# Value products of a sparse and of a memory attention, 256 columns wide in place of 128

## The reference, cut to what matters

```python
def _dsa(...):                      # sparse attention: 8 heads of 128, 2 key-value heads
    ...
        logits = jnp.where(valid[:, :, None, None, :], logits, -jnp.inf)
        p = jax.nn.softmax(logits, axis=-1).astype(v.dtype)
        o = jnp.einsum('bqgrk,bqkgd->bqgrd', p, vg)
...
def _memory_attn(...):              # memory attention: 4 heads of 256 over 256 memory rows
    ...
    logits = jnp.einsum('bthd,bmhd->bhtm', q, k).astype(jnp.float32)
    p = jax.nn.softmax(logits, axis=-1).astype(v.dtype)
    o = jnp.einsum('bhtm,bmhd->bthd', p, v)
```

## Time and profile before

| | us |
|---|---|
| median of 3 runs | 1372.25 (1372.23 to 1376.3) |
| the profiled execution | 1372.86 |
| its span (first to last instruction) | 1371.0 |
| PE busy | 1292.2 (94% of the span) |
| DVE, ACT, POOL busy | 636.5, 636.3, 416.4 |
| sparse attention's steps, about 736 to 853 | 160 value records |
| memory attention's steps, about 974 to 1029 | 128 value records |

### The profile page before, as it was taken

The page is one execution under the profiler, slowest core; times in us unless marked ns, Lnnn a source line. Parts: engine busy times, 40 slices in busy tenths (PEclk is TensorE's granted clock), DMA queues, the critical chain, the costliest instruction groups (busy, mean ns, idle before and its releaser), DMA issues.

```text
span 1371.0 us, 16957 instructions
## 1 busy us (share of the span) xinstructions
PE 1292.2 (94%) x6321; PEld 1000.1 (73%) x6321; DVE 636.5 (46%) x1414; ACT 636.3 (46%) x1107; POOL 416.4 (30%) x211
## 2 busy tenths in 40 slices
PE   5999989889989999999999998999899999999996
PEld 4798666467768767776877786888787777777674
DVE  3265353643320135237897444314334133678785
ACT  5453534353552647445333545333434323477772
POOL 4273232024663421333333222444105431100003
PEclk9999999999999999999999999999999999999999
DMA  5233333133444221222322111342107430799945
GB/s 165 66 115 100 120 119 109 50 101 115 147 119 168 74 80 32 62 77 66 104 85 72 52 54 55 115 153 83 33 1 251 180 151 20 306 409 409 420 185 202
DMA packets 76461, 179.13 MB, mean 131 GB/s; under 512 B 11200, under 2 KB 22774, under 8 KB 69718
## 3 DMA queue, kind: packets, MB, share of 16 engines
q1 hardware_dynamic: 68672, 164.96, 35.1%
q0 software_dynamic: 2592, 8.40, 1.6%
q10 hardware_dynamic: 5110, 4.62, 1.2%
HBM read 152.79 MB, written 25.17 MB: 130 GB/s over the span
## 4 chain that ended last, share of the span: by engine, by line
PE 71%; DVE 8%; ACT 3%; issue 3%; POOL 1%; DMA 0%; DVEq 0%; ACTq 0%; POOLq 0%
PE ps L1064 17%; PE ps L1065 17%; PE ps L1066 17%; PE ps L1602 4%; PE ps L1470 1%; PE ps L1453 1%; PE ps L1586 1%; PE ps L1230 1%; DVE mix_lo L2557 1%; DVE work L2788 1%; PE ps L1426 1%; DVE best L2786 1%; PE ps L1573 1%; PE ps L1498 1%; PE ps L1460 1%
## 5 line engine op out<-in xcount | busy, mean ns | idle before, releaser
L931 POOL TENSOR_TENSOR w_lo<-raw,w_hi 128x1024 fp32r<-128x1024 f32 (+1 forms) x158 | 377.8, 2405 | 733.5 <-ACT w_hi L1829 724.8
L1064 PE MATMUL ps<-w_hi,act_hi 128*128 128x512 f32 (+1 forms) x560 | 234.2, 418 | 5.5 <-DVE probT_m L3224 2.3
L1829 ACT ACTIVATE w_hi<-raw 128x1024 fp32r<-128x1024 f32 (+1 forms) x158 | 159.9, 1033 | 170.0 <-PE ps L1066 161.5
L1065 PE MATMUL ps<-w_lo,act_hi 128*128 128x512 f32 (+1 forms) x560 | 219.7, 392 | 0.0
L1066 PE MATMUL ps<-w_hi,act_lo 128*128 128x512 f32 (+1 forms) x560 | 219.1, 391 | 0.0
L1064 PE MATMUL ps<-w_hi,mix_hi 128*128 128x512 f32 x320 | 131.9, 412 | 4.9 <-DVE mix_lo L2557 3.6
L1064 PEld LDWEIGHTS ps<-w_hi,act_hi 128*128 128x128 f32 (+1 forms) x560 | 104.7, 187 | 43.2 <-issue 12.5
L1066 PE MATMUL ps<-w_hi,mix_lo 128*128 128x512 f32 x320 | 127.0, 397 | 0.0
L1065 PE MATMUL ps<-w_lo,mix_hi 128*128 128x512 f32 x320 | 126.9, 397 | 0.0
L1066 PEld LDWEIGHTS ps<-w_hi,act_lo 128*128 128x128 f32 (+1 forms) x560 | 104.4, 186 | 25.1
L1065 PEld LDWEIGHTS ps<-w_lo,act_hi 128*128 128x128 f32 (+1 forms) x560 | 104.6, 187 | 24.4 <-issue 1.8
(11 more groups left out here) (477 smaller groups left out, 2116.1 us busy)
## 6 DMA issues: line engine op xcount, KB each, us to landing
raw<-in_w_in SPq DMA_DIRECT2D x92, 512.0 KB, 3.6
gu<-in_w_gate SPq DMA_DIRECT2D x16, 1024.0 KB, 7.7
gu<-in_w_up SPq DMA_DIRECT2D x16, 1024.0 KB, 10.0
dn<-in_w_down SPq DMA_DIRECT2D x16, 1024.0 KB, 10.2
x_rows<-zeros SPq DMA_DIRECT2D x16, 512.0 KB, 4.9
raw<-in_w_out SPq DMA_DIRECT2D x16, 512.0 KB, 4.5
raw<-in_w_mem_kv SPq DMA_DIRECT2D x16, 512.0 KB, 3.8
xe<-x_rows SPq DMA_DIRECT2D x15, 512.0 KB, 10.4
```

The costliest lines, as they stand in the source:

```text
L931: pool.tensor_tensor(lo[:, 0:a], raw[:, g % RAW_SLOTS, 0:a], hi[:, 0:a].bitcast(F32), ALU.subtract).then_inc(*POOL.done(("w_lo", g)))
L1064: pe.matmul(dst, l_hi, r_hi, start=start, stop=False, skip_group_check=skip)
L1065: pe.matmul(dst, l_hi, r_lo, start=False, stop=False, skip_group_check=skip)
L1829: nc.scalar.activation(split_slot(g)[0][:, 0:a], raw[:, g % RAW_SLOTS, 0:a], ACTF.Copy).then_inc(*ACT.done(("w_hi", g)))
```

## The change

Two turns now share one value product, 256 columns wide.

- In the sparse attention the order of turns becomes the one of `turn_of`: pairs of heads, and within a pair row block 0 of both heads, row block 1 of both, and so on. Turns j = 2m and 2m + 1 are the two heads of pair m // 4 at row block m mod 4. Both have the same key-value head, so the same value block is the weight for both. The value product m stands in step 2m + 4, where the one of turn 2m + 1 stood; odd steps have none.
- `d_probT` becomes two buffers of two turns each, and bank 7 holds two heads by two row blocks; ACT copies it out every second value product (line 2253 of the new file).
- In the memory attention the order of turns stays. The value product of two neighbouring row blocks of a head is issued where the one of the odd row block stood; the even one's step issues nothing on PE. `m_probT` becomes two buffers of two turns each.
- `mix_dsa` of two heads is laid in when a pair of heads ends.

The multiplications and the shape of scores, transposes, exponentials and divisions are the same ones.

```diff
@@ -297,14 +297,14 @@
     n = NT * DSA_H
     steps = []
     for j in range(n + 3):
-        steps += [[("dsa_values", j - 3)] * (j >= 3) + [("dsa_turn", j - 2)] * (2 <= j < n + 2) + [("dsa_scores", j)] * (j < n)]
+        steps += [[("dsa_values", j // 2 - 2)] * (j >= 4 and j % 2 == 0) + [("dsa_turn", j - 2)] * (2 <= j < n + 2) + [("dsa_scores", j)] * (j < n)]
     done, ended, fresh = [], False, 0
     dense = item("gate01", "w_o01", "gate10")
     for step in [x for s in spread(steps, [[p] for p in dense[:-4]]) for x in s]:
         order += [step]
         ended = ended or step == ("part", "w_o01", KC // 2 - 1, NT - 1)
         if step[0] == "dsa_values" and step[1] % NT == NT - 1:
-            done += [("mix_dsa", step[1] // NT)]
+            done += [("mix_dsa", 2 * (step[1] // NT) + i) for i in range(2)]
             fresh = 2
         elif ended and step[0] == "dsa_turn":
             if done and (len(done) > 1 or not fresh):
@@ -484,7 +484,7 @@
         dv = sb("dv", [P, NT, 256], SC + 49.5)
         d_mask = sb("d_mask", [P, 1280], SC + 53.5)
         rel = sb("rel", [P, 2, SEQ], SC + 58.5)
-        d_probT = sb("d_probT", [P, 2, SEQ], SC + 58.5)
+        d_probT = [sb(f"d_probT{i}", [P, NT, 2, P], SC + at) for i, at in enumerate((58.5, 68.5))]
         d_sq = sb("d_sq", [P, 2, 512], SC + 62.5)
         ik2 = sb("ik2", [P, NT, P], SC + 66.5)
         d_prob = sb("d_prob", [P, 3, SEQ], SC + 62.5)
@@ -503,7 +503,7 @@
         mem_lo = sb("mem_lo", [P, KC, MEM], SC + 28, F32R)
         mqT = sb("mqT", [P, 8, SEQ], SC + 41.5)
         m_prob = sb("m_prob", [P, 3, MEM], SC + 57.5)
-        m_probT = sb("m_probT", [P, 2, MEM], SC + 60.5)
+        m_probT = [sb(f"m_probT{i}", [P, 2, 2, P], SC + at) for i, at in enumerate((60.5, 70.5))]
 
         zeros = sb("zeros", [P, 256], SC + 71.75)
         xs_ffn = sb("xs_ffn", [P, NT, D], SC)
@@ -873,7 +873,7 @@
                         sp.dma_start(mem_vals, mv_new[:, :, :].rearrange("p c n -> p (c n)")).then_inc(mem_spilled, 16)
                     if names[g] == ("mem_q0", 0):
                         sp.wait_ge(mem_spilled, 32)
-                        sp.wait_ge(*PE.after("d_O", NT * DSA_H - 1))
+                        sp.wait_ge(*PE.after("d_O", NT * DSA_H // 2 - 1))
                         sp.wait_ge(*DVE.after("mix_lo", "dsa", DSA_H - 1))
                         sp.dma_start(mkT[:, :, :].rearrange("p c n -> p (c n)"), mem_keys).then_inc(mem_back, 16)
                         sp.dma_start(mv[:, :, :].rearrange("p c n -> p (c n)"), mem_vals).then_inc(mem_back, 16)
@@ -1447,7 +1447,7 @@
                                         [("dqn", n, t) for t in range(NT)])
 
             def dsa_scores(j):
-                h, t = divmod(j, NT)
+                _, t, h, _ = turn_of(j)
                 n = P * (t + 1)
                 claim(4 + j % 2, (DVE, ("d_max", j)))
                 pe.matmul(ps[:, 4 + j % 2, 0:n], dqT[:, h, P * t:P * t + P], dkT[:, h // DSA_G, 0:n], start=True,
@@ -1456,20 +1456,21 @@
             def dsa_turn(j):
                 pe.wait_ge(*DVE.after("d_norm", j))
                 claim(6, (ACT, ("d_PT", j)))
-                for b in range(j % NT + 1):
+                for b in range(turn_of(j)[1] + 1):
                     tr = pe.transpose(ps[:, 6, P * b:P * b + P], d_prob[:, j % 3, P * b:P * b + P], ident[:, :])
                 tr.then_inc(*PE.done(("d_PT", j)))
 
-            def dsa_values(j):
-                h, t = divmod(j, NT)
-                g = h // DSA_G
-                pe.wait_ge(*ACT.after("d_PT", j))
-                if t == 0:
-                    claim(7, (ACT, ("d_out", h)))
+            def dsa_values(m):
+                p, t = divmod(m, NT)
+                g = 2 * p // DSA_G
+                for i in range(2):
+                    pe.wait_ge(*ACT.after("d_PT", 2 * m + i))
+                if t % 2 == 0:
+                    claim(7, (ACT, ("d_out", p, t // 2)))
+                dst = ps[:, 7, :].rearrange("p (i u n) -> p i u n", i=2, u=2)[:, :, t % 2, :]
                 for b in range(t + 1):
-                    mm = pe.matmul(ps[:, 7, P * t:P * t + P], dv[:, b, P * g:P * g + P], d_probT[:, j % 2, P * b:P * b + P],
-                                   start=(b == 0), stop=(b == t))
-                mm.then_inc(*PE.done(("d_O", j)))
+                    mm = pe.matmul(dst, dv[:, b, P * g:P * g + P], d_probT[m % 2][:, b, :, :], start=(b == 0), stop=(b == t))
+                mm.then_inc(*PE.done(("d_O", m)))
 
             def mem_prepare(part):
                 if part == "k":
@@ -1509,14 +1510,18 @@
 
             def mem_values(j):
                 h, t = divmod(j, NT)
-                pe.wait_ge(*ACT.after("m_PT", j))
+                if t % 2 == 0:
+                    return
+                for i in range(2):
+                    pe.wait_ge(*ACT.after("m_PT", j - 1 + i))
                 for c in range(2):
                     bank = MEM_BANKS[2 * h + c]
-                    if t == 0:
+                    if t == 1:
                         claim(bank, (DVE, ("mix_lo", "mem", 2 * h + c)))
                     for b in range(2):
-                        mm = pe.matmul(ps[:, bank, P * t:P * t + P], mv[:, b, 2 * P * h + P * c:2 * P * h + P * (c + 1)],
-                                       m_probT[:, j % 2, P * b:P * b + P], start=(b == 0), stop=(b == 1))
+                        mm = pe.matmul(ps[:, bank, P * (t - 1):P * (t + 1)].rearrange("p (i n) -> p i n", i=2),
+                                       mv[:, b, 2 * P * h + P * c:2 * P * h + P * (c + 1)],
+                                       m_probT[j // 2 % 2][:, b, :, :], start=(b == 0), stop=(b == 1))
                 mm.then_inc(*PE.done(("m_O", j)))
 
             def r_turn(t):
@@ -2228,27 +2233,29 @@
                 nc.scalar.activation(mix_hi[:, c, :], ps[:, bank, :], ACTF.Copy).then_inc(*ACT.done(("mix_hi", tag, c)))
 
             def dsa_scores(j):
-                n = P * (j % NT + 1)
+                n = P * (turn_of(j)[1] + 1)
                 act.wait_ge(*DVE.after("d_nmax", j))
                 nc.scalar.activation(d_prob[:, j % 3, 0:n], d_prob[:, j % 3, 0:n], ACTF.Exp, bias=sm[:, 1, j:j + 1],
                                      scale=float(P) ** -0.5, accum_out=sm[:, 2, j:j + 1]).then_inc(*ACT.done(("d_exp", j)))
 
             def dsa_turn(j):
-                n = P * (j % NT + 1)
+                _, t, _, i = turn_of(j)
                 act.wait_ge(*PE.after("d_PT", j))
-                if j >= 2:
-                    act.wait_ge(*PE.after("d_O", j - 2))
-                nc.scalar.activation(d_probT[:, j % 2, 0:n], ps[:, 6, 0:n], ACTF.Copy).then_inc(*ACT.done(("d_PT", j)))
-
-            def dsa_values(j):
-                h, t = divmod(j, NT)
-                if t == NT - 1:
-                    act.wait_ge(*PE.after("d_O", j))
-                    nc.scalar.activation(dqT[:, h, :], ps[:, 7, :], ACTF.Copy).then_inc(*ACT.done(("d_out", h)))
+                if j >= 4:
+                    act.wait_ge(*PE.after("d_O", j // 2 - 2))
+                nc.scalar.activation(d_probT[j // 2 % 2][:, 0:t + 1, i, :], ps[:, 6, 0:P * (t + 1)].rearrange("p (b n) -> p b n", n=P),
+                                     ACTF.Copy).then_inc(*ACT.done(("d_PT", j)))
+
+            def dsa_values(m):
+                p, t = divmod(m, NT)
+                if t % 2:
+                    act.wait_ge(*PE.after("d_O", m))
+                    nc.scalar.activation(dqT[:, 2 * p:2 * p + 2, P * (t - 1):P * (t + 1)], ps[:, 7, :].rearrange("p (i n) -> p i n", i=2),
+                                         ACTF.Copy).then_inc(*ACT.done(("d_out", p, t // 2)))
 
             def mix_dsa(h):
                 act.wait_ge(*PE.after("acc", "w_o01", NT - 1))
-                act.wait_ge(*ACT.after("d_out", h))
+                act.wait_ge(*ACT.after("d_out", h // 2, 1))
                 nc.scalar.activation(mix_hi[:, h, :], dqT[:, h, :], ACTF.Copy).then_inc(*ACT.done(("mix_hi", "dsa", h)))
 
             def mem_scale(part):
@@ -2277,9 +2284,10 @@
 
             def mem_turn(j):
                 act.wait_ge(*PE.after("m_PT", j))
-                if j >= 2:
-                    act.wait_ge(*PE.after("m_O", j - 2))
-                nc.scalar.activation(m_probT[:, j % 2, :], ps[:, 6, 0:MEM], ACTF.Copy).then_inc(*ACT.done(("m_PT", j)))
+                if j >= 4:
+                    act.wait_ge(*PE.after("m_O", j // 2 * 2 - 3))
+                nc.scalar.activation(m_probT[j // 2 % 2][:, :, j % 2, :], ps[:, 6, 0:MEM].rearrange("p (b n) -> p b n", n=P),
+                                     ACTF.Copy).then_inc(*ACT.done(("m_PT", j)))
 
             def mem_values(j):
                 h, t = divmod(j, NT)
@@ -2812,7 +2820,7 @@
                         scaled_heads(("dqn", n, t), dq[:, t, 512 * n:512 * n + 512], ss[:, 4, a + 4 * t:a + 4 * t + 4], 4)
 
             def dsa_max(j):
-                t = j % NT
+                t = turn_of(j)[1]
```

(2 more changed lines are left out.)

## The result

Over 15 executions each on the same chip the median is 1377.25 us (1374.86 to 1380.06) with the change and 1374.52 us (1370.91 to 1376.3) without it. The ratio is 1.0026 with a 95% interval of 1.0017 to 1.0035, or 3.6 us slower on 1374.5 (2.3 to 4.8); the two means lie 3.7 us apart, the two medians 2.7. The profiled execution took 1376.84 us, its span is 1375.0 us against 1371.0 before.

The account below looks back on a forecast made before the run. PE, busy for 94% of the span, was taken as the bound. Memory attention +3.1 and sparse attention +1.7 gave +4.8 us on 1372.86; with the profiled execution 0.6 above the median, 1377.1, range 1372.8 to 1380.5.

Parts of the forecast that it names:

- The products: Value products of both attentions: columns set the pace, so wider records save only 0.3 us in memory, 0.2 in sparse attention.
- The rival by which instructions set the pace: Wide value records cost like narrow ones: 1361 us, or 1364 by the skill page; 0.05 together with waits that vanish.
- The memory attention: Its stage: even steps grow by 6.4 us, odd steps give back 3.3, so +3.1 us.
- 7 and 15: Memory attention steps after a head's end without a dense part: nothing comes back, PE stands for about 1.8 us.
- The sparse attention: Its stage: most odd steps get their time back, three places don't; with the products' -0.2 it is +1.7 us.
- The term for the table loads: Sparse attention: the copy of turn 11 stands on ACT behind two table loads and a sigmoid; +0.9 us.
- the term for POOL: Sparse attention: divisions slowed by POOL's low halves lose their covering product in odd steps; +1.0 us, ends 0 and 2.
- the steps with `mix_dsa`: Sparse attention steps 26 to 32, holding five of six division waits: no change, ends -1.0 and +1.3 us.
- a later stage that gets shorter: Sign of being wrong: a stage behind the two attentions gets shorter by what these two lose.
- The rival of the clock: New stands in the memory attention lower the granted clock: one fall gives 1378.5 us, two 1379.9; chance 0.22.
- More cover than I count: Memory attention's odd steps recover nearer 4.0 us than 3.3, sparse attention even or half a microsecond ahead: 1374.5; chance 0.30.
- Bank 7: Sparse attention: turns of two heads wait for each other through bank 7, 0.6 us eight times; given next to nothing.

Follow-up runs that it names:

- e3: The changed kernel with its order, buffers and places, but every wide product made as two narrow ones in both attentions; ratio 1.0028 to the kernel before.
- e1: The kernel before with the change in the memory attention alone; ratio 1.0034 to the kernel before.
- e4: e1 with the dense parts of `gate20` laid one behind step 0, two behind step 1, one behind each even step; ratio 0.9982 to the kernel before.
- e9: e4 with the dense part behind step 16 moved behind step 18; median 1369.31 us against 1373.43 for the kernel before, ratio 0.9975.
- e6: e1 with each wide product issued as two halves, one step apart, the last one whole; ratio 1.0007 to the kernel before.
- e2: The kernel before with the sparse attention's part of the change alone; ratio 1.0006 to the kernel before.

## Why the prediction was right

Predicted were 1377.1 us and a loss of 4.8; measured were 1377.25 and 3.6 by the ratio, whose interval reaches 4.8. The direction held, and so did the mechanism in the memory attention. Two things are luck. The absolute time fits within 0.2 us only because two misses cancel: the three executions that I built on had a median of 1372.25, the fifteen have 1374.52, 2.3 more, and the loss is 1.2 less than forecast. And the sparse attention's +1.7 is met by a comparison that the clock distorts; at the same places of low clock it is 0.8, as said below. The size lies just below the 0.3% that I had called the edge of what can be told from none; with its interval of 0.17 to 0.35% it was told.

**The products.** Predicted 0.2175 us for a record of 256 columns and 0.5 us saved. In after it is 1.72 / 8 = 0.215, and e3 against after gives 0.5 us in the memory stage alone, 0.2 more than priced. The rival by which instructions set the pace is out: it needed under 0.19. With it goes, for this kernel, the estimate from the Trainium skill's page "TensorE: Matmul & The Clock Gate" (section "Back-to-back issue gap").

**The memory attention.** Predicted +3.1, measured +3.0 (58.57 against 55.55), +2.9 in e1. The even steps grew by 6.3 us in all (forecast 6.4), and the odd ones gave back 3.2 (forecast 3.3). Step by step: steps 3 and 5 stand 1.53 us each where 0.64 stood, 7 and 15 stand 1.72 (predicted 1.8), step 11 stands 0.33 (0.4 by "about 0.5 comes back"), step 17 0.56, and 9 and 13 don't stand. The reason for it, that an odd round lost 0.88 us of cover and only a dense part ahead makes up for that, was tested from two sides: e4 and e9 put parts there and the stands fell to 0.34 us or less, e6 put half a product of 0.87 us there and they shrank by 0.9, 0.95 and 1.5. e3 ruled the width out. Of steps 7 and 15 the chain is seen whole in after. Timelines of ACT and DVE, steps 6 and 7:

```profile
999.16 1.09 ACT L2233 ACTIVATE mix_hi<-ps 128x512 fp32r<-128x512 f32 x2 [0.82 <-PE ps L1522]
...
999.79 1.29 DVE L2565 SCALAR_TENSOR_TENSOR mix_lo<-ps,mix_hi 128x512 fp32r<-128x512 f32 x2 [3.31 <-ACT mix_hi L2233]
...
1001.52 0.35 DVE L2849 TENSOR_SCALAR m_prob<-m_prob,sm 128x256 f32<-128x256 f32 x1
```

From `mix_hi` at 999.16 to the transposes at 1001.92 it is 2.76 us, as in the earlier trace rows (2.77), and it moved with the product.

**The sparse attention.** Predicted +1.7, and the two profiled executions differ by 1.7 (117.70 against 116.01). That this fits is luck: in after the clock was low near 745 and 845, in before near 745 and 785. Against e1, with the old sparse attention and the pattern of after, the loss is 0.8 in after and 0.7 in e2. The term for the table loads came out: the stand of 1.93 us became 2.95, +1.0 for +0.9 predicted. Its parts didn't. From the first scores PE reaches this place 1.25 us earlier than before (predicted 2.1) and is through it 0.2 earlier (predicted 1.2); both are off by 0.9 to 1.0, which cancels. The rows of after are these, ACT, then PE, then a division beside POOL's low half:

```profile
778.24 1.28 ACT L1842 ACT_TABLE_LOAD   x1
...
783.29 1.10 PE L1472 MATMUL ps<-d_probT,dv 128*128 128x256 f32 x4 [2.95 <-ACT d_probT L2246]
...
787.42 0.55 PE L1460 MATMUL ps<-ident,d_prob 128*128 128x128 f32 x3 [0.45 <-DVE d_prob L2849]
...
786.43 0.94 DVE L2849 TENSOR_SCALAR d_prob<-d_prob,sm 128x384 f32<-128x384 f32 x1
...
784.76 2.39 POOL L931 TENSOR_TENSOR w_lo<-raw,w_hi 128x1024 fp32r<-128x1024 f32 x1 [9.36 <-ACT w_hi L1834]
```

The term that was mis-sized is that of POOL, +1.0 for two or three stands. After shows one such stand, 0.45 us behind a division of 0.94 us beside POOL, and even that one isn't the change's: e1, with the sparse attention of before, has it as well. Rows of e1, PE and DVE, and the window 784 to 787, then PE in before at the same place:

```profile
786.48 0.44 PE L1460 MATMUL ps<-ident,d_prob 128*128 128x128 f32 x2 [0.53 <-DVE d_prob L2846]
...
785.06 1.36 DVE L2846 TENSOR_SCALAR d_prob<-d_prob,sm 128x256 f32<-128x256 f32 x1
...
784.00:787.00 3.00, 2.47 (x13) 1.84 (x12) 2.04 (x5) 1.22 (x5) 2.27 (x1) 1.00 0.00 0
...
787.21 0.38 PE L1460 MATMUL ps<-ident,d_prob 128*128 128x128 f32 x2
```

In both kernels POOL makes a low half beside this division, in e1 from 783.89 to 786.27. In before the clock was 0.53 from 784 to 787; PE came to these transposes late, and the division, 0.75 us there, was done. In e1 it was 1.00, and PE came early and stood. So a stretch at the lower level costs less where it takes the place of a stand, and the term for POOL is near zero here. The waits in the steps with `mix_dsa` came out at 5.5 us (the 8.2 of the waits less 2.3 for the first turn and this 0.45) for 5.2, inside the ends of -1.0 and +1.3 around my zero. With 0 in place of the 1.0 for POOL my sum for the sparse attention is +0.7, and with the 3.1 of the memory attention +3.8, close to the 3.6 measured.

**The rest of the program.** I took it as unchanged, and had named a later stage that gets shorter as a sign of being wrong. In the profiled executions it is 0.7 us shorter: unchanged instructions are 1.3 us later already at 740, ahead of both stages, and behind the memory attention 2 us of the loss come back. What differs there is where the granted clock was low. Windows with the columns of the earlier trace rows, of before:

```profile
276.00:290.00 14.00, 10.77 (x78) 7.35 (x77) 4.99 (x16) 6.12 (x12) 2.35 (x1) 1.00 0.13 40
...
1100.00:1130.00 30.00, 27.90 (x130) 22.60 (x129) 10.15 (x16) 9.40 (x13) 9.50 (x4) 0.94 0.41 158
```

And of after, the third over the memory stage:

```profile
276.00:290.00 14.00, 10.81 (x71) 7.29 (x70) 4.62 (x14) 5.39 (x11) 2.35 (x1) 0.88 0.22 68
...
1100.00:1136.00 36.00, 33.90 (x163) 27.78 (x162) 10.84 (x17) 10.59 (x14) 14.21 (x7) 1.00 0.47 173
...
976.00:1036.00 60.00, 50.43 (x246) 41.24 (x246) 22.79 (x79) 24.51 (x67) 4.71 (x2) 1.00 0.02 5
```

No part of the change lies near 276 or 1100, and the clock was lower near 276 in after and near 1100 in before. Over all of it the granted clock is 0.985 in both executions. So I don't put the 0.7 us down to the change. Why the falls land where they do stays open.

**The rival of the clock** had 0.22 and didn't come true in the memory stage: through seven stands of 0.3 to 1.7 us the granted clock was 1.00. A stand costs its own length there.

**The other rivals.** *More cover than I count* (1374.5, 0.30) fell in the memory stage, where 3.0 of the 3.1 us came. The 3.6 us of the ratio lie between it and the forecast; what is missing to 4.8 is about what the sparse attention falls short of its +1.7 at a like clock, 0.9 us. *Bank 7* didn't show: PE waits at the value product of the sparse attention once, for the copy to `d_probT`.

## What to carry to other kernels

Price an operation by what it covers as well as by its own time. Putting two products into one saves little where columns set the pace, and it takes the cover from every second round of a softmax pipeline whose round trip (2.01 us here) is only just hidden. Once work has been moved, lay the independent parts anew: into the rounds that became short, and not where their readout stands ahead of a division that the next round waits for. Against the kernel before the best placing was worth 3.7 us in the stage, and 2.7 of them came without the wide products.
